# One layer of a recurrent and attention mixer on one core: gate products in 64x64 quarters of the array, scores for four heads at a time, transposes behind later units

## The reference

```
h = rms_norm(x); proj = h @ w_in                  # 1024 x 2560: xr, yg, q, k, v of 512 each
xr = causal_conv4(xr)
r, i = sigmoid(xr_head @ w_a + b_a), sigmoid(xr_head @ w_i + b_i)    # 8 heads of 64x64
log_a = -8 r softplus(-lambda); u = sqrt(1 - exp(2 log_a)) * (i * xr)
h_t = exp(log_a) h_(t-1) + u_t ;  y_lru = h * gelu(yg)
q, k = rms_norm per head of 64 ; y_attn = causal attention with a linear bias, 8 heads
x = x + concat(rms_norm(y_lru), rms_norm(y_attn)) @ w_out
x = x + (gelu(gate) * val) @ w_down,  gate, val = causal_conv3(rms_norm(x) @ w_up)    # 2816 each
```

## Time and profile before

| | us |
|---|---|
| median of 3 runs | 294.61 (294.53 to 294.75) |
| the profiled execution, its time | 294.54 |
| its span | 292.8 |
| TensorE busy | 287.6 |
| VectorE busy | 242.1 |
| ScalarE busy | 200.8 |
| GpSimd busy | 11.8 |

### The profile page before, as it was taken

How to read it: one execution, slowest core, us unless ns; L and a number is a source line. 1 busy time by engine, 2 the same in 40 slices (tenths; PEclk the granted TensorE clock), 3 DMA queues, 4 the chain that set the end, 5 groups by cost and what they waited for, 6 DMA issues and landing times.

```text
span 292.8 us, 4964 instructions
## 1 busy us (share of the span) xinstructions
PE 287.6 (98%) x1626; PEld 248.3 (85%) x1626; DVE 242.1 (83%) x443; ACT 200.8 (69%) x378; POOL 11.8 (4%) x29
## 2 busy tenths in 40 slices
PE   6999999999999999999999999999999999999996
PEld 6588999898788899888888888888888888888885
DVE  2798797898899777999977888888788888888875
ACT  4884498989695489788676666676666666776540
POOL 4000000900000000000000000000000000000000
PEclk9999999999999999999999999999999999999999
DMA  7999942142156703473747444454746444200004
GB/s 273 428 420 421 406 152 72 75 143 65 81 189 241 282 9 130 159 282 150 286 144 270 163 161 178 159 218 143 286 143 244 185 158 153 120 0 0 0 0 146
DMA packets 8111, 52.23 MB, mean 178 GB/s; under 512 B 928, under 2 KB 1312, under 8 KB 2080
## 3 DMA queue, kind: packets, MB, share of 16 engines
q1 hardware_dynamic: 7920, 51.50, 47.3%
q0 software_dynamic: 176, 0.53, 0.5%
HBM read 50.98 MB, written 1.05 MB: 178 GB/s over the span
## 4 chain that ended last, share of the span: by engine, by line
PE 95%; DMA 2%; ACT 1%; SPq 0%; DVE 0%; issue 0%
PE bank L1360 26%; PE bank L1040 16%; PE bank L1041 15%; PE bank L1044 15%; PE bank L1364 14%; DMA x_tok<-in_x_dram 2%; PE bank L1327 1%; PE bank L1335 1%; PE bank L1149 1%; PE bank L1263 1%; PE bank L1176 1%; PE bank L1090 1%; PE bank L1297 1%; PE bank L1143 1%; PE bank L1184 1%; PE bank L1183 1%
## 5 line engine op out<-in xcount | busy, mean ns | idle before, releaser
L688 DVE TENSOR_TENSOR w_lo<-raw,w_hi 128x1024 fp32r<-128x1024 f32 x93 | 110.9, 1221 | 6.9 <-ACT w_hi L361 5.9
L361 ACT ACTIVATE w_hi<-raw 128x1024 fp32r<-128x1024 f32 x85 | 86.8, 1059 | 4.9 <-PE bank L1044 4.5
L1360 PE MATMUL bank<-h_both,w_hi 128*128 128x512 f32 x336 | 83.7, 391 | 0.0
L1360 PEld LDWEIGHTS bank<-h_both,w_hi 128*128 128x128 f32 x336 | 61.7, 188 | 11.8
L1364 PEld LDWEIGHTS bank<-h_both,w_lo 128*128 128x128 f32 x336 | 45.8, 191 | 3.3
L1364 PE MATMUL bank<-h_both,w_lo 128*128 128x256 f32 x336 | 46.9, 283 | 0.0
L603 ACT ACTIVATE tanh_a<-bank 128x256 f32<-128x256 f32 x44 | 16.8, 381 | 40.3 <-PE bank L1364 40.0
L1040 PE MATMUL bank<-w_hi,act_hi 128*128 128x512 f32 (+1 forms) x90 | 34.9, 388 | 0.0
L1041 PE MATMUL bank<-w_lo,act_hi 128*128 128x512 f32 (+1 forms) x90 | 34.9, 387 | 0.0
L1044 PE MATMUL bank<-w_hi,act_lo 128*128 128x512 f32 (+1 forms) x90 | 34.6, 385 | 0.0
L611 ACT ACTIVATE xc<-ygate,par 128x256 f32<-128x256 f32 x44 | 26.2, 595 | 3.6 <-DVE ygate L965 3.6
(11 more groups left out here) (168 smaller groups left out, 402.0 us busy)
## 6 DMA issues: line engine op xcount, KB each, us to landing
raw<-in_stream_dram SPq DMA_DIRECT2D x47, 1024.0 KB, 4.8
x_tok<-in_x_dram SPq DMA_DIRECT2D x2, 512.0 KB, 5.1
out_dram<-x_tok SPq DMA_DIRECT2D x3, 256.0 KB, 2.1
p_T<-in_gates_dram POOLq DMA_DIRECT2D x1, 512.0 KB, 9.7
out_dram<-x_tok SPq DMA_DIRECT2D x2, 128.0 KB, 2.0
par<-in_params_dram SPq DMA_DIRECT2D x1, 117.0 KB, 6.6
mix_g<-in_params_dram POOLq DMA_DIRECT2D x1, 4.0 KB, 5.6
```

The lines of the kernel that those rows point to most:

```text
L361: act.activation(w_hi[u % RING][:, :], raw_unit(u), ACT.Copy).then_inc(hi_done, 1)
L688: dve.tensor_tensor(w_lo[u % RING][:, :], raw_unit(u), w_hi[u % RING][:, :].bitcast(F32), ALU.subtract).then_inc(lo_done, 1)
L1360: pe.matmul(acc[:, :], whi[:, kc, :], h_both[:, kc, :, :].rearrange("p b t -> p (b t)"), start=kc == 0, stop=False)
```

## The change

- The gate weights are used as 64x64 blocks. Each chunk of 128 channels (two heads) and two gates gives four matmuls on the four quarters of the array. The gate r of the even head goes from the even rows to the even columns, that of the odd head from odd rows to odd columns. For the gate i the columns are crossed: the even head's result lands in partitions 64 to 127, the odd head's in 0 to 63. ScalarE's sigmoid exchanges the partitions again, in two instructions of 64 partitions for each chunk. The order of the chunks is 0, 2, 1, 3; chunks 0 and 2 share two banks, and 1 and 3 two others; r and i are in different banks. All gates wait for the fourth convolution, and ScalarE reads them in pairs of chunks.
- Every head has a place of its own for its probabilities (in `qk_tok`, `v_tok` and `p_T`), and the scores have six places in PSUM (heads 0 to 3 in banks 0 to 3, heads 4 and 5 in banks 0 and 1, heads 6 and 7 in banks 4 and 5). The scores of four heads follow each other.
- TensorE's order: unit 10, scores 0 to 3, units 11, 12 (behind shift(3)), gates, unit 13, scores 4 to 7, unit 14, transposes 0 and 1, unit 15, transposes 2 and 3, unit 16, transposes 4 and 5, unit 17, transposes 6 and 7, units 18, 19.
- ScalarE and VectorE are reordered to match: on ScalarE exps(2) in front of the split of unit 15, exps(4) behind the square, `v_out(1)` in front of `y_to_hi(0)`; on VectorE the shifts in groups of four, lo(15) and lo(16) together behind the convolutions, the row scaling of heads 4 to 7 together, and lo(20) behind the product with ygate.

```diff
--- before.py
+++ after.py
@@ -29,6 +29,7 @@
 AX_X = mybir.AxisListType.X
 
 P = 128
+HALF = P // 2
 D_MODEL = 1024
 SEQ = 256
 LRU_WIDTH = 512
@@ -52,7 +53,6 @@
 RING = 6
 WARM_UP = 10
 F_CUT = 384
-P_SLOTS = 5
 POOL_HEADS = 4
 MASKED = -3.0e38
 KEYS = [P, 2 * P]
@@ -139,8 +139,12 @@
         mix_g = sb("mix_g", [P, KC])
         small = sb("small", [P, 208])
 
-        probs = [qk_tok[:, :, :].rearrange("p a b -> p (a b)")[:, SCORES * j:SCORES * (j + 1)]
-                 for j in range(P_SLOTS)]
+        def flat(t):
+            return t[:, :, :].rearrange("p c t -> p (c t)")
+
+        prob_home = (*((flat(qk_tok), SCORES * j) for j in range(5)),
+                     (flat(v_tok), 0), (flat(p_T), 7 * SCORES), (flat(v_tok), SCORES))
+        probs = [tile[:, at:at + SCORES] for tile, at in prob_home]
 
         conv_g = [xc[:, j, :] for j in range(2)]
         conv_v = [xc[:, 2 + j, :] for j in range(2)]
@@ -151,9 +155,6 @@
 
         w_gate = p_T[:, 4:8, :].rearrange("p h s -> p (h s)")[:, 0:2 * LC * P].rearrange(
             "p (g c j) -> p g c j", g=2, c=LC)
-
-        def flat(t):
-            return t[:, :, :].rearrange("p c t -> p (c t)")
 
         x_norm = [flat(decay), flat(gate_i)]
         h_plain = xc
@@ -239,7 +240,7 @@
         Q_ACC, K_ACC, X_ACC = bank[0:2], bank[2:4], bank[4:8]
         Y_ACC, V_ACC = bank[2:4], bank[4:6]
         QK_T = bank[0:4]
-        S_BANK, P_BANK = bank[0:2], bank[6:8]
+        S_BANK, P_BANK = (*bank[0:4], *bank[0:2], *bank[4:6]), bank[6:8]
         Y_SUM, A_SUM, A_ACC = bank[5][:, 0:TT], bank[5][:, TT:2 * TT], (bank[4], bank[2])
 
 
@@ -263,6 +264,13 @@
 
             tile, at = (bank[2 + kc % 4], kc // 4) if m == 0 else (bank[6 + kc // 4], kc % 4)
             return tile[:, P * at:P * (at + 1)]
+
+        GATE_ORDER = (0, 2, 1, 3)
+
+        def gate_acc(g, c):
+
+            at = SEQ * (1 - c // 2)
+            return X_ACC[2 * (c % 2) + g][:, at:at + SEQ]
 
         def f_at(m, kc):
 
@@ -347,7 +355,7 @@
             for h in range(POOL_HEADS):
                 pool.wait_ge(row_rec_done, h // 2 + 1)
                 for m in range(TT):
-                    part = probs[h % P_SLOTS][:, KEY_AT[m]:KEY_AT[m] + KEYS[m]]
+                    part = probs[h][:, KEY_AT[m]:KEY_AT[m] + KEYS[m]]
                     pool.tensor_scalar(part, part, row_rec[:, h, m:m + 1], None, ALU.mult).then_inc(probs_scaled, 1)
 
 
@@ -452,7 +460,7 @@
                 act.wait_ge(shifted, h + 1)
                 for m in range(TT):
                     part = slice(KEY_AT[m], KEY_AT[m] + KEYS[m])
-                    act.activation(probs[h % P_SLOTS][:, part], probs[h % P_SLOTS][:, part], ACT.Exp, scale=-1.0,
+                    act.activation(probs[h][:, part], probs[h][:, part], ACT.Exp, scale=-1.0,
                                    bias=neg_max[:, h, m:m + 1],
                                    accum_out=row_sum[:, h, m:m + 1]).then_inc(probs_done, 1)
 
@@ -485,19 +493,18 @@
             act.activation(lam_u, lam_z, ACT.Exp, scale=-1.0).then_inc(lam_exp, 1)
             exps(0)
             exps(1)
-            his(15)
+            exps(2)
             conv_first(3)
-            exps(2)
             exps(3)
-            his(16)
-
-            for c in range(LC):
-                act.wait_ge(gates_done, c + 1)
-                act.activation(gate_r[:, c, :], X_ACC[c][:, 0:SEQ], ACT.Sigmoid,
-                               bias=par[:, B_A + c:B_A + c + 1])
-                act.activation(gate_i[:, c, :], X_ACC[c][:, SEQ:2 * SEQ], ACT.Sigmoid,
-                               bias=par[:, B_I + c:B_I + c + 1]).then_inc(gates_read, 1)
-            exps(4)
+            his(15, 16)
+
+            for n, c in enumerate(GATE_ORDER):
+                act.wait_ge(gates_done, 2 * (n // 2) + 2)
+                act.activation(gate_r[:, c, :], gate_acc(0, c), ACT.Sigmoid, bias=par[:, B_A + c:B_A + c + 1])
+                for rows, swapped in ((slice(0, HALF), slice(HALF, P)), (slice(HALF, P), slice(0, HALF))):
+                    ins = act.activation(gate_i[rows, c, :], gate_acc(1, c)[swapped, :], ACT.Sigmoid,
+                                         bias=par[rows, B_I + c:B_I + c + 1])
+                ins.then_inc(gates_read, 1)
             act.wait_ge(log_c_done, 1)
             act.wait_ge(gates_read, LC)
             for c in range(LC):
@@ -508,6 +515,7 @@
                     p_out(c)
             act.wait_ge(decay_done, LC)
             act.activation(flat(gate_r), flat(decay), ACT.Square).then_inc(a2_done, 1)
+            exps(4)
             exps(5)
             p_out(2)
             p_out(3)
@@ -536,9 +544,9 @@
                 act.activation(v_tok[:, m, :], V_ACC[m][:, :], ACT.Copy).then_inc(v_ready, 1)
 
             v_out(0)
+            v_out(1)
             act.wait_ge(y_done, 1)
             y_to_hi(0)
-            v_out(1)
             y_to_hi(1)
             act.activation(y_sq, flat(ygate), ACT.Square).then_inc(y_sq_done, 1)
             y_to_hi(2)
@@ -777,11 +785,9 @@
                 dve.wait_ge(scores, h + 1)
                 if h == 0:
                     dve.wait_ge(dist_done, TT)
-                if h >= P_SLOTS:
-                    dve.wait_ge(pT, h - P_SLOTS + 1)
                 for m in range(TT):
                     part = slice(KEY_AT[m], KEY_AT[m] + KEYS[m])
-                    ins = dve.tensor_tensor_reduce(probs[h % P_SLOTS][:, part], S_BANK[h % 2][:, part],
+                    ins = dve.tensor_tensor_reduce(probs[h][:, part], S_BANK[h][:, part],
                                                    neg_dist[:, part], -slope(h), 3.4e38, ALU.add, ALU.min,
                                                    neg_max[:, h, m:m + 1])
                 ins.then_inc(shifted, 1)
@@ -811,14 +817,13 @@
             los(14)
             shift(0)
             shift(1)
-            conv_rest(2)
-            los(15)
             shift(2)
             shift(3)
+            conv_rest(2)
+            row_reciprocals(0)
             conv_rest(3)
-            row_reciprocals(0)
-            los(16)
             row_reciprocals(2)
+            los(15, 16)
 
 
             dve.wait_ge(lam_exp, 2)
@@ -834,22 +839,22 @@
             link(dve.scalar_tensor_tensor(lam_p, lam_s, 2.0, lam_p, ALU.mult, ALU.add))
             dve.tensor_scalar(log_c, lam_p, -LRU_C, None, ALU.mult).then_inc(log_c_done, 1)
             shift(4)
+            shift(5)
+            shift(6)
+            shift(7)
             dve.wait_ge(gates_read, LC)
             dve.wait_ge(conv_done, LC)
             dve.tensor_tensor(flat(gate_i), flat(gate_i), flat(xc), ALU.mult).then_inc(lru_in, 1)
-            shift(5)
-            row_scale(4)
             los(17, 18)
 
             dve.wait_ge(a2_done, 1)
             dve.scalar_tensor_tensor(flat(tanh_a), flat(gate_r), 1.0, flat(tanh_a), ALU.add,
                                      ALU.mult).then_inc(one_m_a2, 1)
+            row_scale(4)
             row_scale(5)
-            shift(6)
-            shift(7)
             row_scale(6)
             row_scale(7)
-            los(19, 20)
+            los(19)
 
             dve.wait_ge(root_done, 1)
             dve.wait_ge(lru_in, 1)
@@ -860,6 +865,7 @@
             dve.wait_ge(ygate_done, 2)
             dve.wait_ge(scan_done, LC)
             dve.tensor_tensor(flat(ygate), flat(tanh_a), flat(ygate), ALU.mult).then_inc(y_done, 1)
+            los(20)
 
             def y_to_lo(c):
                 dve.wait_ge(y_hi, c + 1)
@@ -1146,7 +1152,7 @@
             def score_part(h, m):
 
                 c, rows_h = h // 2, slice(HEAD_DIM * (h % 2), HEAD_DIM * (h % 2 + 1))
-                return pe.matmul(S_BANK[h % 2][:, KEY_AT[m]:KEY_AT[m] + KEYS[m]],
+                return pe.matmul(S_BANK[h][:, KEY_AT[m]:KEY_AT[m] + KEYS[m]],
                                  q_T[rows_h, c, P * m:P * (m + 1)], k_T[rows_h, c, 0:KEYS[m]],
                                  start=True, stop=True)
 
@@ -1154,8 +1160,10 @@
 
                 if h == 0:
                     pe.wait_ge(qkT_read, LC)
-                else:
-                    pe.wait_ge(shifted, h)
+                elif h == 4:
+                    pe.wait_ge(shifted, 2)
+                elif h == 6:
+                    pe.wait_ge(gates_read, 2)
                 for m in range(TT):
                     for j in range(2):
                         ins = score_part(h + j, m)
@@ -1173,16 +1181,18 @@
                 if h >= 2:
                     pe.wait_ge(pT_read, h - 1)
                 for b in range(SCORES // P):
-                    ins = pe.transpose(P_BANK[h % 2][:, P * b:P * (b + 1)], probs[h % P_SLOTS][:, P * b:P * (b + 1)],
+                    ins = pe.transpose(P_BANK[h % 2][:, P * b:P * (b + 1)], probs[h][:, P * b:P * (b + 1)],
                                        ident[:, :])
                 ins.then_inc(pT, 1)
 
             def gates_product(c):
 
-                pe.wait_ge(conv_done, c + 1)
```

(27 more changed lines are left out.)

## The result

| | before | after |
|---|---|---|
| median, us | 294.75 (294.45 to 295.22, 11 runs) | 296.38 (295.00 to 296.66, 11 runs) |
| ratio of after to before, 95% interval | | 1.0038 [1.0027, 1.0049] |
| profiled execution, us | 294.54 | 295.05 (span 293.3) |

The change makes the kernel slower by 0.4%; the forecast was 294.9 with a range of 294.1 to 296.8. The median hides that the runs of after fall into two groups with nothing between them: 295.00 to 295.15 (5 runs, mean granted clock of TensorE over the execution 1.000, the profiled one among them) and 296.38 to 296.66 (6 runs, clock 0.994), 1.45 us apart. I call them the quicker and the slower group. The ratio's middle, 1.0038, lies between the groups, which stand at 1.001 and 1.006. So there are two things to explain: 0.5 us on the profiled execution, where 0.3 was forecast, and 1.45 us in six runs of eleven.

What follows compares the result with a forecast made beforehand. TensorE and VectorE were taken to bound the kernel together: TensorE's queue gets 2.1 us shorter, but VectorE enters lo(21) 0.3 later, so 294.54 + 0.3 = 294.84, median 294.9 us, range 294.1 to 296.8.

Steps and rivals of the forecast that it cites:

- What bounds the kernel: TensorE, busy 98%, and VectorE arrive together at 86.5 us; TensorE's saving counts only as far as VectorE enters lo(21) earlier.
- the load's 0.17 us: Weight load for a_sums stood 0.17 us until VectorE wrote k_T; taken as showing how far ahead VectorE is.
- Gates: TensorE's gates: four quarters run at once, 1.97 us with overhead and entry, instead of 3.46.
- Rival B: Gate quarters go two at a time, gates 3.80 us, first transpose another 1.73 later: 296.6 us; chance 0.25.
- Scores and transposes: TensorE: two score pairs in a row take 0.86 + 0.65 = 1.51 us; first transpose at 58.93, 1.73 later than before.
- ScalarE: Four extra gate reads at 0.38 each, +1.5 us; p_out(0) at 59.45, square at 62.72, root near 70.1, +0.4.
- The extra reads are covered: ScalarE's extra reads vanish in its stall of some 1.2 us for the transpose before p_out(0), leaving +0.48.
- VectorE: Starts the product with the root at 71.2, lo(20) behind the ygate product, enters lo(21) at 78.40 instead of 78.10: +0.3.
- Rival C: VectorE's stretch does not hold TensorE, so the 2.1 us saved arrive: 292.5 us; chance 0.08.
- Sum: Profiled execution 294.54 + 0.3 = 294.84 us; median 294.9.
- The clock: The forecast also fails if TensorE's granted clock falls while it stands 1.7 us before a_sums; no chance or price given.
- A: The forecast itself: four quarters at once, VectorE's stretch sets the end; own range 294.4 to 295.5 us; chance 0.60.

Runs made afterwards that it cites:

- 1: Changed kernel with VectorE's lo(19) moved ahead of the wait for the square and lo(20) ahead of the product with the root; 294.40 us, ratio 0.9990 to before.
- 6: Changed kernel with gate i read whole (exchange left out) and ScalarE's p_out(0) and p_out(1) moved behind the square; 293.76 us, ratio 0.9969 to before.
- 8: Changed kernel with lo(19) and lo(20) moved into VectorE's waits and lo(21) ahead of the first y_to_lo; 293.66 us, ratio 0.9966 to before.
- 9: Kernel before with only lo(21) moved ahead of the first y_to_lo on VectorE; 294.79 us, ratio 1.0006 to before.
- 4: Kernel before with only the gates in quarters and the crossed reads, scores, transposes and order otherwise as before; 297.98 us, ratio 1.0107 to before.
- 5: Changed kernel with gate i read whole, exchange of partitions left out, 8 ScalarE reads instead of 12; 295.52 us, ratio 1.0031 to before.
- 2: Changed kernel with spare TensorE products filling its waits, two before y_sums and six before a_sums; 295.09 us, ratio 1.0011 to before.
- 10: Changed kernel with lo(19) to lo(21) in VectorE's gaps and the gates as 8 full products with 8 whole reads; 294.83 us, ratio 1.0003 to before.
- 3: Changed kernel with the gates as 8 full 128x128 products, gate i read whole; 298.00 us, ratio 1.0089 to before.
- 7: Changed kernel with gate i's two half reads each into their own partitions, not crossed (exchange left out); one execution, 295.43 us.

## Why the prediction was right

**What bounds the kernel.** Right. TensorE at 98% with one wait was bound, and VectorE was a tenth of a microsecond from it. In experiments 1, 6 and 8 VectorE's entry moved and the end moved with it, TensorE's products unchanged (in 8 until TensorE itself was last); in 9 it moved with TensorE's queue as before, and nothing came. Both bounds at the same place is what the load's 0.17 us had said.

**Gates.** Right: 1.96 us for 1.97, 1.89 up to the next unit. Rival B falls, in after and in 4. By the Trainium skill, "TensorEngine Tiling (Array Packing)", Restrictions and Gotchas, the even-row and the odd-row quarter of one gate could not write one bank at once; the trace has four passes starting together in that pattern, and `gate_acc` gives those two quarters one bank, in different partitions. The trace disagrees with that rule as far as this pattern goes.

**Scores and transposes.** Right: two pairs took 1.51 us up to the next unit, as summed; the first transpose came at 59.05 for 58.93, of which 0.09 was there at 42.16 already.

**ScalarE.** The step that was mis-sized, without a consequence: a read costs 0.49, not 0.38, so they ended at 57.4, not 56.1, and the stall of some 1.2 us before `p_out(0)` was nearly nothing (last tanh and transpose ready within a tenth of each other). So one of the signs named in advance, ScalarE idle for over 1 us before `p_out(0)`, did not appear. (The sum there also has 59.45 where 58.93 + 0.49 is 59.42, which changes nothing.) `p_out(0)` came at 59.58 for 59.45, the square at 62.87 for 62.72, the root at 70.25 for 70.1. "The extra reads are covered" held with hardly a tenth to spare; that the time came out as summed is partly luck, for a read only a little dearer would have moved `p_out(0)` and what follows. 5 shows that the reads cost nothing there, 4 what they cost where the cover is missing.

**VectorE.** Right: product 71.34 for 71.2, lo(20) filling the gap, lo(21) at 78.55 for 78.40. The gain in TensorE's queue of about 2 us turned into the wait ahead of `a_sums`, 1.38 us (forecast 1.7), and that ahead of `y_sums`, 0.23 (0.5): the lead was 1.8 at the attention product, where 1.9 was summed. Rival C falls by the same row.

**Sum.** At clock 1.000 the change cost 0.51 us on the profiled execution for 0.3 forecast, and 0.36 by the medians (295.11 for 294.75). Of the missing 0.2, 0.15 stands at lo(21) already, 0.09 of it this trace's later entry at 42 us; the rest is no more than what separates executions.

**What the sum did not hold.** The clock. The forecast named its fall during TensorE's wait as a thing that would break it, and gave it no chance and no price; it came in six executions of eleven and cost 1.45 us, so that the median is 296.38 and not 295.1. That 296.38 lies inside the range is luck: the forecast's own rival, A, ended at 295.5, and the range reached to 296.8 only for quarters that run two at a time, which did not happen. Right are the queues and the 295.1 of the quicker group; of the 1.6 us by which the median rose, 1.3 come from a term that the sum put at nothing. That it comes from TensorE's stands is shown by filling them (2): 0 of 11. It agrees that none was seen where VectorE's order took the stand away (8: 0 of 6, 10: 0 of 11) nor in the 59 executions of before that ran beside the experiments. With a stand of 1.38 to 1.42 us there were 6 of 11 (after), 4 of 6 (3), 1 of 7 (5) and 0 of 1 (7), with 2.12 us 2 of 4 (4); with 0.9 us 0 of 11 (1) and 0 of 6 (6). Where the clock falls was seen in the profiles of 3 and 4; for after it is inferred, since its profile has clock 1.000 (a mean of 0.994 over 294.8 us is 1.8 us of full clock, as much as 3 lost in its windows). What decides which execution falls stays open, as does why 5, with the same stand, fell so seldom. It ran on another chip than 1 to 4, and whether the chip matters was not tried; 6 and 8 ran on that same chip, so that their 0 of 6 weigh little.

## What to carry to other kernels

When an engine is at 98% and a second arrives only 0.1 us behind it, a saving on the first needs a change of the second's queue in the same edit: here about 2 us of TensorE's time gave +0.5 us with the change's own order of VectorE, and -1.0 us once VectorE's splits stood in its waits for ScalarE. The waits to fill were found in the profile of the changed kernel; the one that before had gave nothing (9). A wait that TensorE gains is to be priced with the clock behind it, and over several executions, since a single profile may show the quicker group.

## What the runs showed of the hardware

- Four 64 by 64 quarters of the array run at once with fp32 operands, also when two of them with different rows write different partitions of one bank: 32 passes of 256 columns in 1.96 us, against 3.62 us for the same gates as 16 full passes.
- ScalarE's reads of 256 columns from a bank start 0.36 us apart when all use the 128 partitions, 0.48 when two halves follow each other, and 0.49 from a whole read to a half that crosses to the other partitions (0.37 when it does not cross).
- Within 0.8 us behind a stand of 1.4 us in a queue otherwise full, TensorE's clock went from 2.4 to 1.2 GHz in the profile of 3; by the mean clock it fell in some executions and not in others of the same kernel. In experiment 4 it did so as TensorE resumed from a stand of 2.12 us; the window is one of its profile, as above:

```profile
60.00:65.00 5.00, 5.00 (x34) 5.00 (x33) 4.38 (x12) 4.99 (x14) 0.00 (x0) 0.72 0.02 3
```

Its two groups lie only 0.9 us apart. In this profile, one of the slower group, TensorE has no wait ahead of `a_sums`. So presumably the quicker executions had one there, which took up a part of the lower clock's cost; none of them has a trace.
